# The level products of the HGRN mixer's last six chunks: from GpSimd to VectorE

## The reference

```python
log_f = jnp.log(f)                       # f is the forget gate, k = 1 - f
bc = jnp.cumsum(chunkify(log_f), axis=3)
diff = bn[:, :, :, None, :] - bn[:, :, None, :, :]
decay = jnp.exp(jnp.where(causal[:, :, None], diff, -jnp.inf))
scores = jnp.einsum('bhtk,bhsk,bhtsk->bhts', qn, kn, decay)
o = (jnp.einsum('bhts,bhsv->bhtv', scores, vn)
     + jnp.einsum('bhtk,bhkv->bhtv', qn * jnp.exp(bn), state))
```

## Time and profile before

| | us |
|---|---|
| median of 3 runs | 5791.25 (5775.8 to 5795.71) |
| the profiled execution | 5785.04 |
| its span, first to last instruction | 5783.4 |
| DVE busy | 2567.3 (44%) |
| ACT busy | 2169.1 (38%) |
| PE busy | 4733.8 (82%) |
| POOL busy | 677.6 (12%) |
| stages 10 to 15, the ones changed | 4955.7 to about 5446 |

### The profile page before, as it was taken

One profiled execution on the slowest core, in us unless ns is written; L12 is line 12 of the kernel. 1 busy time (PEld: TensorE's weight loads), 2 busy tenths in 40 slices (PEclk: granted clock), 3 DMA queues, 4 the chain that ended last, 5 costly groups with the idle time before them and its releaser, 6 DMA issues. The chain is left out here.

```text
span 5783.4 us, 60201 instructions
## 1 busy us (share of the span) xinstructions
PE 4733.8 (82%) x20922; PEld 3405.8 (59%) x20922; DVE 2567.3 (44%) x5295; ACT 2169.1 (38%) x4039; POOL 677.6 (12%) x724
## 2 busy tenths in 40 slices
PE   3994999982488889989798999968788887776689
PEld 2883777772477777767545888844344454444444
DVE  3111444444444444444111101127888887776324
ACT  3011333333223333333111101123777768677522
POOL 2001111100000000000000000002222323344300
PEclk7997999985667777687899999965587877876789
DMA  3514666652100000000232122110000000000032
GB/s 111 169 63 156 207 216 220 213 183 100 43 21 21 21 21 11 21 21 3 96 92 81 62 79 79 54 56 11 26 17 17 17 33 17 34 17 33 28 127 87
DMA packets 225807, 417.14 MB, mean 72 GB/s; under 512 B 34840, under 2 KB 97976, under 8 KB 225336
## 3 DMA queue, kind: packets, MB, share of 16 engines
q1 hardware_dynamic: 225504, 413.29, 21.2%
HBM read 291.55 MB, written 121.65 MB: 71 GB/s over the span
## 5 line engine op out<-in xcount | busy, mean ns | idle before, releaser
L2355 PE MATMUL ds_big<-ds_ikT,ds_iqT 64*128 64x512 f32 (+3 forms) x640 | 435.3, 784 | 76.0 <-ACT ds_iqT L2327 54.5
L2858 POOL TENSOR_TENSOR ds_E<-ds_bT 128x256 f32<-128x256 f32 x112 | 73.6, 657 | 3115.1 <-ACT ds_bT L2827 2932.8
L290 DVE COPY g_stage<-g_acc 128x512 f32<-128x512 f32 (+2 forms) x96 | 61.6, 642 | 785.1 <-PE g_acc L278 785.1
L276 PE MATMUL g_acc<-g_ws_hi,second_hT_hi 128*128 128x512 f32 (+1 forms) x1024 | 384.9, 376 | 11.6 <-DVE g_ws_lo L311 11.6
L277 PE MATMUL g_acc<-g_ws_lo,second_hT_hi 128*128 128x512 f32 (+1 forms) x1024 | 384.6, 376 | 0.0
L278 PE MATMUL g_acc<-g_ws_hi,second_hT_lo 128*128 128x512 f32 (+1 forms) x1024 | 384.5, 376 | 0.0
L304 ACT ACTIVATE g_stage<-g_acc 128x512 f32<-128x512 f32 (+2 forms) x96 | 53.7, 559 | 844.7 <-PE g_acc L278 844.7
L546 PE MATMUL mm_big<-mm_gw_hi,mm_ghT_hi 128*128 128x512 f32 (+1 forms) x768 | 317.9, 414 | 42.3 <-PEq L132 42.3
L2419 DVE TENSOR_SCALAR_CACHE_REDUCE ds_eq<-ds_hi,ds_num 128x2048 uint16<-128x2048 uint16 (+13 forms) x224 | 331.3, 1479 | 25.9 <-issue 3.9
L548 PE MATMUL mm_big<-mm_gw_hi,mm_ghT_lo 128*128 128x512 f32 (+1 forms) x768 | 299.0, 389 | 0.0
L547 PE MATMUL mm_big<-mm_gw_lo,mm_ghT_hi 128*128 128x512 f32 (+1 forms) x768 | 298.9, 389 | 0.0
(11 more groups left out here) (500 smaller groups left out, 10349.8 us busy)
## 6 DMA issues: line engine op xcount, KB each, us to landing
mm_ghT_hi<-turned SPq DMA_DIRECT2D x96, 512.0 KB, 4.0
mm_ghT_lo<-turned SPq DMA_DIRECT2D x96, 512.0 KB, 5.5
proj<-g_stage SPq DMA_DIRECT2D x160, 256.0 KB, 2.0
g_w<-in_w_in SPq DMA_DIRECT2D x80, 256.0 KB, 4.1
proj<-mm_gstage SPq DMA_DIRECT2D x80, 256.0 KB, 5.1
mm_x<-proj SPq DMA_DIRECT2D x64, 256.0 KB, 3.9
mm_graw<-in_w_in SPq DMA_DIRECT2D x40, 256.0 KB, 6.3
po_m<-mixed SPq DMA_DIRECT2D x16, 640.0 KB, 4.7
```

What stands on the lines that cost most here:

```text
L276: pe.matmul(sums, hT.hi[:, k, tile], wt.hi[:, k, 0:width], start=(k == 0), stop=False)
L2355: pe.matmul(big[:, n % 2, 0:wd], iqT[:, h], b.ikT[:, x:x + wd], start=True, stop=True)\
```

## The change

In chunks 10 to 15 the two tilde multiplications of each of the seven levels are issued by DVE at place 7.5 + 2l of DVE's list, with the same wait for the level's exponentials and the same signals. In the other chunks POOL does them as before. Everything else keeps its engine and its place. A new constant sets the first chunk of the new kind.

```diff
+LATE = 10
...
+    def tilde(eng, l):
+
+        e0, e1 = halves(E[:, l % 2], l)
+        eng.wait_ge(s.h_exps, l + 1)
+        eng.tensor_tensor(e0, e0, halves(kT[:], l)[0], ALU.mult).then_inc(s.tilde, 1)
+        eng.tensor_tensor(e1, e1, halves(qT[:], l)[1], ALU.mult).then_inc(s.tilde, 1)
...
             yield (7.5 + 2 * l) / N
-            tilde(l)
+            if i < LATE:
+                tilde(pool, l)
...
         for l in range(LEVELS):
+            if i >= LATE:
+                yield (7.5 + 2 * l) / N
+                tilde(dve, l)
             if l:
                 yield (9.3 + 2 * l) / N
                 pick(l - 1)
```

More of the change, by code:

```diff
@@ L2859, in diffs @@
             pool.tensor_tensor(e1, b1, joint(l), ALU.subtract).then_inc(s.diffs, 1)
[L2861 to L2865, removed]
         yield 6 / N
```

## The result

| | us |
|---|---|
| before | 5786.78 median of 18 runs (5775.8 to 5799.34) |
| changed | 5811.93 median of 18 runs (5798.57 to 5830.37) |
| changed to before | 1.0041, 95% interval 1.0032 to 1.0051 |
| profiled execution's span, changed | 5804.1 (before 5783.4) |

The change made the kernel slower, by about 24 us by the ratio (the medians differ by 25). The forecast was 5800 with a range of 5768 to 5822, so the time lies inside the range, and nearer to the middle of rival 2 (5820) than to the forecast.

The account below looks back on a forecast made before the run. DVE's own instruction list was taken to bound the stages between round 11 and the last pick. Added pairs, collisions and waits, less stretches given back, summed to +13.7 us on 5785.04, 5798.7, stated as 5800, range 5768 to 5822.

Parts of the forecast that it names:

- rival 2: Stages 10 to 15: DVE's list takes the whole price, nothing absorbs the early levels; +35 us, 5820; chance 0.2.
- the prediction's signs: Expected in the profile: among others, DVE busy up by 20 to 28 us over the six stages, POOL's down by 68.
- the sum: Forecast lengthening of stages 10 to 15: +3.5, +3.3, +2.2, +1.7, +1.7 and +1.3, together +13.7 us.
- the forecast's own range: Whole kernel: 5788 to 5812 around the forecast of 5800, for the forecast's own 0.45 chance.
- Price of a pair: On DVE, a level's two tilde multiplications take 0.77 us, 5.4 us per chunk, 32 us in all.
- Collisions with POOL: DVE's new instructions meet POOL's diffs and are stretched, taken as 0.4 us per chunk.
- Stretches given back: DVE instructions no longer stretched by POOL's tilde: 2.3, 2.5, 2.2, 2.0, 2.3 and 0.8 us in stages 10 to 15.
- The added wait: DVE waits for each level's exponentials; mostly absorbed by idle time in stages 12 to 14, at worst 9 us in all.
- Late levels: Stages 12 to 14, levels 3 to 6: pairs 3.1 us plus collisions, less some 1.7 us of stretches, +1.6 each.
- Rival 1: The chain of a level, not DVE's list, sets the pace: faster by 18 us, 5767; chance 0.2.

Follow-up runs that it names:

- e4: Kernel before, with DVE in chunks 10 to 15 also doing multiplications of tilde's shapes into a spare tile nobody reads; 1.0058 of before.
- e3: The change for levels 3 to 6 alone, levels 0 to 2 staying on POOL; 1.0036 of the kernel before.
- e2: The change for levels 0 to 2 alone, levels 3 to 6 staying on POOL; 1.0007 of the kernel before.
- e1: The change with DVE's tilde of level 5 moved from place 17.5 to 17.35 and level 6 from 19.5 to 19.0; 1.0029 of the kernel before.
- e6: The change with only DVE's tilde of level 5 moved, from place 17.5 to 17.35, ahead of the closing part; 1.0015 of the kernel before.
- e5: The change, with POOL in chunks 10 to 15 doing multiplications of the old tilde shapes into an unread spare tile; 1.0050 of the kernel before.
- e8: The kernel before with tilde of levels 0 to 2 on DVE in chunks 12 to 15 only; 1.0002 of before.

## Why the prediction was right, and which terms were off

The mechanism was right: DVE's list sets the pace from the first level to the last pick, and work put on it is paid there. e4 shows it (no one waits for that work's result, and it costs 29 us), and e3 with e2 shows where. DVE's busy time rose by 21 us, as the prediction's signs had it (20 to 28). The size was less good: the stages grew by 21.3 us where the sum had 13.7, and that 5811.93 lies just inside the forecast's own range, 5788 to 5812, is luck. Point by point:

- **Price of a pair, 0.77 us.** Right where undisturbed.
- **Collisions with POOL, 0.4 us per chunk.** About right in stages 10 to 14: 2.7 us over the five (2.4 in the second profile) where the forecast had 2.0. In stage 15 they were 5.1 us in one profile and 0.9 in the other, with stage lengths of 72.6 and 71.4. The prediction named the diffs as what the tilde would meet. The larger part of the 7.8 us is another instruction of POOL, L2588 of attention (1.3 us each, some 4 us in all), of which the prediction says nothing. That ke and qe come earlier, which the prediction had seen ("some 3 us earlier in POOL's time"), hurts the tilde of level 5 in stage 15, and in the other stages only once that tilde is moved ahead of the closing part (e1, e6).
- **Stretches given back, 12.1 us.** About right. The stretches of all DVE instructions but the new ones, counted against each instruction's usual undisturbed time, fell from 38 to 23 us: 15 in place of 12 (13 in the second profile, counted the same way). With the collisions the net is 7 us, where the forecast had 9.7. e5, which puts POOL's load back, undoes this give-back: DVE's busy time rises by 16 us there, more than half of it on the tilde instructions.
- **The added wait.** Right in its effect in stages 12 to 14: the waits of the earlier trace rows are gone. In stages 13 and 14 waits of 0.4 to 0.9 us for the exponentials stand at levels 0 and 1 in their place; in stage 12, for which the prediction worked out 0.5 and 1.5 us, there is none. The early pairs cost little there (e2, e8).
- **Late levels, +1.6 a stage.** This is the step that failed. "This is within the sum" holds for DVE's own list only. The list puts the tilde of level 5 behind the closing part, PE stood 3.6 us in stage 13, and DVE later waited for PE: DVE's idle time behind the pick of level 3 rose from 0.7 to 7.4 us over the six stages, +6.7. e6 took it away by one place number, and the six stages fell by 4.4 us. I had seen PE's wait for the pick of level 4 and looked for a longer one at level 6; it came at level 5. The granted clock of these stretches, 0.50 to 0.84 where it had been 0.85 to 1.00, is in no term of the prediction, and it made the late waits longer.
- **Rival 1**, the level chain, is out: e2 would have been at 0.998, and its interval starts at 0.9998. e8's stages 12 to 15 are 3.4 us shorter than before; that may be a small remainder of it or scatter. **Rival 2** is nearer in size and has the reason wrong: the stretches were given back and the early pairs mostly absorbed.

Put into the sum, 0.7 for collisions in stages 10 to 14, -3 for the stretches and +6.7 for the late waits make it about 18, to which stage 15's collisions add something; the six stages have 21.3. The rest is no larger than the 3.9 us by which stages of unchanged code differed, so no cause can be named for it. In how it falls on stages (stage 13 at +4.9, where POOL's L2588 now stretches two L2423 from 0.16 to about 1.2 us) I see no rule.

## What to carry to other kernels

When work goes to an in-order engine that paces a stage, its length is only the first term. Look at what stands right ahead of the new place in the list, and at what the engine that waits for it has queued behind: the slip can come back as a wait on the first engine. And when an engine is relieved, its next instructions start earlier; find what they then run beside, above all when the two engines hold each other up. Before a wait is put down to an order of work alone, compare the granted clock of the same stretch in both kernels, and take a second profile: here the collisions of one kernel were 7.8 us in one execution and 3.3 in the other.

## What the runs showed of the hardware that I had not expected

Two VectorE instructions of 0.42 us and two GpSimd ones of 1.25 us, all with two SBUF inputs, the first of each started within 0.05 us of the other, took turns: 1.27, 1.50, 1.45 and 1.48 us, 2.95 us from the first start to the last end (e1_places). Small instructions suffer as much as long ones: L2429, 128x16, took 1.17 us behind a GpSimd multiplication and 0.16 undisturbed, while L2419 (16-bit data, one tensor input) kept to within 0.01 us at every size in stages 10 to 14. The Trainium skill's rule ("SBUF — State Buffer", section "SBUF: two separate sides") of an exclusive hold for a whole instruction describes each such row. How much of it reaches the time only the runs tell: 56 us of GpSimd load put back in the six stages made VectorE busy for 16 us longer and the stages 6.7 us longer (e5_poolload).

The same chain of TensorE work, from the level 5 products to L2696 in stage 13, took 3.3 us at a granted clock of 1.00 and 6.1 us at 0.50, and the clock of this stretch differed between kernels whose TensorE work is the same.
